# Scan of a two-layer block on one core: the local outputs are multiplied behind the first state step, and VectorE evacuates them behind its first state

## The reference

```python
def wkv_scan(r, w, k, v, kk, a, s0, reverse):
    def step(s, inp):
        r_t, w_t, k_t, v_t, kk_t, a_t = inp
        sa = jnp.einsum('bhij,bhj->bhi', s, -kk_t)
        s = (s * w_t[:, :, None, :] + sa[..., None] * (kk_t * a_t)[:, :, None, :]
             + v_t[..., None] * k_t[:, :, None, :])
        return s, jnp.einsum('bhij,bhj->bhi', s, r_t)
...
    yf, sf = wkv_scan(r, wf, kf, v, kk, af, s0[0], False)
    yb, sb = wkv_scan(r, wb, kb, v, kk, ab, s0[1], True)
    y = yf + yb
```

## Time and profile before

| | |
|---|---|
| median of 3 runs | 2883.44 us (2880.14 to 2884.04) |
| span of the profiled execution | 2886.6 us, 56801 instructions |
| TensorE busy | 2817.8 us, 98% of the span |
| VectorE busy | 1865.0 us, 65% |
| ScalarE busy | 1347.8 us, 47% |
| GpSimd busy | 226.0 us, 8% |
| mean granted TensorE clock | 0.994 of full speed |

### The profile page before, as it was taken

How to read it: one execution, slowest core, us unless ns; L and a number is a source line. 1 busy time by engine, 2 the same in 40 slices (tenths; PEclk the granted TensorE clock), 3 DMA queues, 4 the chain that set the end, 5 groups by cost and what they waited for, 6 DMA issues and landing times.

```text
span 2886.6 us, 56801 instructions
## 1 busy us (share of the span) xinstructions
PE 2817.8 (98%) x24171; PEld 2382.1 (83%) x24171; DVE 1865.0 (65%) x2553; ACT 1347.8 (47%) x1947; POOL 226.0 (8%) x271
## 2 busy tenths in 40 slices
PE   6999999999999999999999999999999999999998
PEld 3687888888988878888888888888888888888887
DVE  3597886777777676664455566789775555554444
ACT  3222446566655444444444444566544444444443
POOL 1000002333231000000000000133000000000000
PEclk9999999999999999999999999999999999999999
DMA  9997881000001668876656556666556666666664
GB/s 386 369 373 262 273 274 36 8 11 10 8 8 58 209 211 261 260 236 183 189 185 194 191 180 221 189 178 182 172 182 189 191 188 188 191 189 199 189 191 160
DMA packets 470781, 532.30 MB, mean 184 GB/s; under 512 B 22920, under 2 KB 422722, under 8 KB 469634
## 3 DMA queue, kind: packets, MB, share of 16 engines
q1 hardware_dynamic: 464754, 516.13, 55.6%
q0 software_dynamic: 3408, 10.43, 1.1%
q10 hardware_dynamic: 2368, 2.11, 0.3%
HBM read 522.29 MB, written 4.19 MB: 182 GB/s over the span
## 4 chain that ended last, share of the span: by engine, by line
PE 90%; DVE 4%; DMA 2%; ACT 1%; issue 1%; ACTq 0%; SPq 0%; DVEq 0%
PE ps L2489 14%; PE ps L2500 14%; PE ps L2502 14%; PE ps L2501 14%; PE ps L2665 9%; PE ps L2490 7%; PE ps L3015 4%; PE ps L3016 2%; PE ps L2511 2%; PE ps L2512 2%; PE ps L2513 2%; DMA raw<-in_w_mod 1%; PE ps L2693 1%; PE ps L2691 1%; PE ps L2912 1%
## 5 line engine op out<-in xcount | busy, mean ns | idle before, releaser
L1596 DVE TENSOR_TENSOR lo<-raw,hi 128x1024 fp32r<-128x1024 f32 x776 | 948.5, 1228 | 714.7 <-ACT hi L1069 709.4
L1069 ACT ACTIVATE hi<-raw 128x1024 fp32r<-128x1024 f32 x776 | 820.3, 1059 | 1074.1 <-PE ps L2502 603.0
L2500 PE MATMUL ps<-hi,mov 128*128 128x512 f32 x1408 | 553.4, 393 | 3.6 <-DVE mov L1664 3.6
L2502 PE MATMUL ps<-hi,mov 128*128 128x512 f32 x1408 | 549.3, 390 | 0.0
L2501 PE MATMUL ps<-lo,mov 128*128 128x512 f32 x1408 | 549.0, 390 | 0.0
L2500 PEld LDWEIGHTS ps<-hi,mov 128*128 128x128 f32 x1408 | 264.9, 188 | 58.2 <-issue 4.4
L2502 PEld LDWEIGHTS ps<-hi,mov 128*128 128x128 f32 x1408 | 264.9, 188 | 55.9
L2501 PEld LDWEIGHTS ps<-lo,mov 128*128 128x128 f32 x1408 | 265.1, 188 | 53.9
L2489 PE MATMUL ps<-mov,hi 128*128 128x512 f32 x864 | 306.2, 399 | 0.4 <-DVE mov L2419 0.3
L2489 PE MATMUL ps<-hid,hi 128*128 128x512 f32 x704 | 244.3, 394 | 0.0
L2490 PE MATMUL ps<-mov,lo 128*128 128x256 f32 x864 | 242.2, 280 | 0.0
(11 more groups left out here) (448 smaller groups left out, 4248.7 us busy)
## 6 DMA issues: line engine op xcount, KB each, us to landing
raw<-in_w_in SPq DMA_DIRECT2D x184, 512.0 KB, 4.8
raw<-in_w_gate SPq DMA_DIRECT2D x176, 256.0 KB, 2.9
raw<-in_w_up SPq DMA_DIRECT2D x176, 256.0 KB, 3.2
raw<-in_w_down SPq DMA_DIRECT2D x88, 512.0 KB, 3.6
raw<-in_w_ffn_gate SPq DMA_DIRECT2D x176, 256.0 KB, 2.9
raw<-in_w_ffn_up SPq DMA_DIRECT2D x176, 256.0 KB, 3.1
raw<-in_w_ffn_down SPq DMA_DIRECT2D x88, 512.0 KB, 4.4
raw<-in_w_out SPq DMA_DIRECT2D x64, 512.0 KB, 4.0
```

The source lines that it names most:

```text
L1069: act.activation(hi[:, s, :, :], src, ACT.Copy).then_inc(hi_ready, 1)
L1596: dve.tensor_tensor(lo[:, s, :, :], raw_at(ph, i, j)[0], hi[:, s, :, :].bitcast(F32), ALU.subtract)\
L2500: pe.matmul(out, x(k)[:, 0, tokens], w_hi, start=first, stop=False)
L2502: mm = pe.matmul(out, x(k)[:, 1, tokens], w_hi, start=False, stop=last)
```

## The change

The 32 matmuls `Y` of each direction leave their place behind that direction's `B`. Both directions' `Y` (64 matmuls) now stand in the loop of the state chain, behind `st0` of both directions and ahead of `gram(..., 0)`. On VectorE both `Y0` instructions leave their place behind `Bm` and stand behind both instructions of `s0`. No instruction is added or taken away on any engine. The two tables of names follow, so that the semaphore values fit. All of it concerns token units (`q` = 1), of which there are eight.

```diff
@@ pe_names
-        return out + ["Z", "A", "B"] + (["Y"] if q else []) + [f"st{n}" for n in range(1 - q, NC)]
+        return out + ["Z", "A", "B"] + (["st0", "Y"] if q else []) + [f"st{n}" for n in range(1, NC)]
@@ dve_names
-        out += ["AT"] + (["rho2"] if q else []) + ["Bm"] + (["Y0"] if q else [])
-        return out + [f"s{n}" for n in range(1 - q, NC - q)]
+        out += ["AT"] + (["rho2"] if q else []) + ["Bm"]
+        return out + (["s0", "Y0", "s1", "s2"] if q else ["s1", "s2", "s3"])
@@ VectorE, unit
-                    if q and d == 0:
-                        scan_pe[0].wait(dve, (1, "Y"), b)
-                        done(d, dve.tensor_copy(y, ps[:, 3, 0:T]), "Y0")
-                    elif q:
-                        scan_pe[1].wait(dve, (1, "Y"), b)
-                        own(0, "Y0")
-                        done(d, dve.tensor_tensor(y, ps[:, 7, 0:T], y, ALU.add), "Y0")
                 if ahead:
                     front(*following(b, q), "tail")
                 for n in range(1 - q, NC - q):
...
+                    if n == 0 and q:
+                        scan_pe[0].wait(dve, (1, "Y"), b)
+                        done(0, dve.tensor_copy(y, ps[:, 3, 0:T]), "Y0")
+                        scan_pe[1].wait(dve, (1, "Y"), b)
+                        own(0, "Y0")
+                        done(1, dve.tensor_tensor(y, ps[:, 7, 0:T], y, ALU.add), "Y0")
@@ TensorE, unit
-                    if q:
-                        two(d, (q, "Y"), 3, lambda c, hs: tokV[hs, c, :], lambda c, hs: RT[d][hs, c, :],
-                            lambda c, hs: XY[d][hs, c, 1, :], lambda c, hs: tokBQ[d][hs, c, C:2 * C])
...
                         scan_pe[d].done(mm, (q, f"st{n}"))
+                    for d in range(2 if q and n == 0 else 0):
+                        two(d, (q, "Y"), 3, lambda c, hs: tokV[hs, c, :], lambda c, hs: RT[d][hs, c, :],
+                            lambda c, hs: XY[d][hs, c, 1, :], lambda c, hs: tokBQ[d][hs, c, C:2 * C])
                     for done in (OUTPUTS_AT[n] if q else ()):
```

## The result

The changed kernel took 2887.99 us (median of 13 runs, 2884.93 to 2891.14), the kernel before 2881.84 us (13 runs, 2879.55 to 2885.90). The ratio is 1.0020, with a 95% interval of 1.0012 to 1.0028: 5.8 us slower, between 3.5 and 8.1. Each of these two has an interval that just includes 1; the first doesn't. So the change loses a little, in the direction of the forecast of +2.7 us. The profiled execution of the changed kernel had a span of 2883.7 us, shorter than the 2886.6 of the one before: single executions of one kernel differ by several us, and two spans don't settle a few us. The lengths of the unit tails do (from the inversion's last product `Z` to the following unit), since they repeat to 0.01 or 0.02 us from one trace of a kernel to another.

The account below looks back on a forecast made before the run. The prediction took TensorE's order, busy for 98% of the span, to bound the kernel. Its terms, +4.6 - 2.1 - 0.8 + 0.4 + 0.6 = +2.7 us, gave 2886.1 us against the median 2883.44, range 2880 to 2891.

Parts of the forecast that it names:

- Term 1: Ahead of direction 1's st0 in eight token units: TensorE newly waits 0.58 us for Bm, +4.6 us in all.
- Term 2: At st1: TensorE's wait for s0 goes, giving back 2.1 us in seven units and 0.77 in the last.
- Term 3: At output(0) and st2, behind VectorE's later Y0 addition: new waits, +0.4 us in seven units, net 0.64 in the last.
- Rival A: VectorE's addition, norm step and s1 behind Y become the bound in every unit: 10 us slower, 2893.7 us; chance 0.10.
- Rival B: The new pause makes TensorE's clock fall in each token unit: 15 us slower, 2898 us; chance 0.06.
- Rival C: Ahead of direction 1's st0, Bm stays covered, so only gains remain: -1.9 us, 2881.5 us; chance 0.19.

Follow-up runs that it names:

- e2: The changed kernel with direction 1's AT computed a second time on VectorE ahead of Bm in each token unit; 2889.26 us, ratio 1.0023 to the kernel before.
- e4: The changed kernel with direction 0's Y moved between direction 1's B and st0, direction 1's Y behind st0; 2881.86 us, ratio 0.9997 to the kernel before.
- e6: The kernel before with only VectorE's order changed, both Y0 instructions behind s0; 2890.00 us, ratio 1.0013 to the kernel before.
- e7: The changed kernel with seven units' gram between direction 1's B and st0, not behind Y; 2887.56 us, ratio 1.0003 to the kernel before.
- e10: The changed kernel with direction 0's Y kept behind its own B, only direction 1's behind st0; 2888.60 us, ratio 1.0010 to the kernel before.
- e3: The changed kernel with VectorE's group norm step between s0 and the Y0 copy, not ahead of s1; 2885.02 us, ratio 1.0009 to the kernel before.
- e5: The changed kernel with direction 0's Y between direction 1's B and st0, and the norm step between Bm and s0; 2881.23 us, ratio 0.9984 to the kernel before.
- e1: The changed kernel measured again without an edit; 2885.59 us, ratio 1.0007 to the kernel before.

## Why the prediction was right, and where its sizes were off

**What bounds.** Right: a pause of TensorE of 0.33 us more per unit lengthened each tail by 0.33 (e2). The list of waits had one longer entry at the state step than the 4.0 us named there, "issue", 5.3 us, 7 times; it belongs to context units and is 5.3 us, 7 times, after the change too.

**Term 1, the new pause.** Right in place and price: 0.57 us, where the forecast had 0.58 from `unit(7, 0)`. It left out that the second half of `st0` then takes 0.17 us until the next matmul instead of 0.12: 0.05 us a unit.

**Term 2, the pause removed.** Right: `st1` follows at once and takes 0.24 us.

**Term 3, what is late next.** The term mis-sized. I had 0.06 us of `st2` for each inner unit; that was met (0.30 against 0.24). But behind it the outputs are followed by `key_gram`, which waits for the key factor of line 1931, the last link of the same string: 0.52 instead of 0.47 us. That it waits shows in the distances: `key_gram` begins 0.83 us behind the start of line 1931's instruction in block 1 of the changed kernel, e2, e4, e6, e7 and e10 alike, and 0.91 behind it in e3, where the factor comes earlier and the outputs take 0.46. With the 0.05 of term 1, the sum in block 1 is 0.57 + 0.05 - 0.30 + 0.06 + 0.05 = 0.43; the tail says 0.47. The last 0.04 lies behind the start of `key_gram`: from there to `U` it is 1.00 us in the changed kernel and 0.96 before and in e3, so it comes and goes with that wait; why it outlasts it isn't shown. The forecast was 0.58 - 0.30 + 0.06 = 0.34. e3, which takes the norm step out of the string, brings the tail to +0.31, which is 0.57 + 0.05 - 0.30 = 0.32. Block 0, which has no norm step, had no part in term 3 (+0.31), though the forecast counted seven such units. For the last unit I had 0.58 - 0.77 + 0.64 = 0.45; it was 0.48.

**The sum.** +2.7 forecast (2.8 without the rounding of its terms), +3.6 in the traces, +3.3 as the mean of three comparisons (5.8, 2.0 and 2.0 by their ratios). That three such comparisons came out on both sides of the traces' figure is the size of their error, so the time alone supports the direction and the size to about 2 us; the terms are settled by the tails. The median of the first lay 1.9 us above the forecast's 2886.1 and inside the range.

**Rival A.** Not the bound in the inner units, since the gram covers, as the prediction said; but e6 and e7 show how near it is: without a `Y` behind `st0` (e6) both directions' `output(0)` wait, and without the gram behind `Y` (e7) direction 1's waits.

**Rival B.** The granted clock in the stretch with the new pause, 563 to 566 us of the changed kernel:

```profile
563.00:566.00 3.00, 2.59 (x89) 2.45 (x86) 1.91 (x6) 0.00 (x0) 0.00 (x0) 1.00 0.00 0
```

It stayed at the upper level of 2.4 GHz, as it did in every 2 us of the scan in the three traces of the changed kernel and in e2. The Trainium skill's rule cited for this rival (page "TensorE: Matmul & The Clock Gate", section "A second HAM failure mode: psum-queue depth-cycling": small idle times between groups make the clock swing) did not come into play at pauses of this size.

**Rival C.** Out: the wait for line 2076 is there eight times more. It is true only of a kernel in which a `Y` covers the pause (e4).

## What to carry to other kernels

Independent work between two dependent steps is a cover, and moving it opens the place that it leaves: before moving it, name what must be hidden at either end (here 0.57 us for `Bm`, 0.30 for `s0`), and split the work so that each place keeps one piece (e4, e5). Look in the trace for a unit in which the cover is already missing, such as `unit(7, 0)`; its wait is the price, to 0.01 us here. On the engine that evacuates, put what nobody waits for soon (the norm step) into an idle stretch, not into the string on which the next state hangs.

## What the runs showed of the hardware that I had not expected

TensorE has pauses in the inversion for which the profile names no releaser and whose length varies at the same instruction of the program's repeated units. Two rows of the kernel before, the same place in blocks 1 and 2:

```profile
520.01 1.04 PEld L2665 LDWEIGHTS ps<-dirs,lev 64*64 64x64 f32 x32 [1.02 <-issue]
...
577.47 1.04 PEld L2665 LDWEIGHTS ps<-dirs,lev 64*64 64x64 f32 x32 [0.43 <-issue]
```

They are a part of why one execution's span says little: from `U` to `Z`, summed over the sixteen units, the traces of one and the same kernel lay 2.4 us apart (the changed kernel, first trace against e1), while the sum of the tails agreed to 0.04 us. What makes these pauses was not tried.

One thing stays open here. The same sum from `U` to `Z` was 312.1 and 313.2 us in the two traces of the kernel before (the first with the clock's fall in block 6), and 307.2 to 310.0 in the eleven others, e6 and the better versions among them. Two traces are too few to say whether a longer or shorter tail changes the inversion behind it or whether these were executions with longer pauses. The times speak against a gain of that size: over the eleven comparisons of kernels that differ from before, the first one included, they lie on average 0.6 us below what the tails say, with single comparisons off by up to 2.7 us.
